# Experts ranked by count on the chip: four run in three terms on 128 slots, four in plain fp32 on 64 slots

## The reference, cut to what matters

```python
def moe_swiglu(h, w_router, b_router, w_gate, w_up, w_down):
    t = h.reshape(-1, dm)                                    # 256 x 1024
    logits = (t @ w_router).astype(jnp.float32) + b_router
    top_vals, top_idx = lax.top_k(logits, TOP_K)             # TOP_K = 2
    top_w = jax.nn.softmax(top_vals, axis=-1)
    gates = jnp.einsum('nk,nke->ne', top_w, jax.nn.one_hot(top_idx, N_EXPERTS))
    out = jnp.zeros_like(t)
    for e in range(N_EXPERTS):                               # 8
        out = out + gates[:, e:e + 1] * swiglu(t, w_gate[e], w_up[e], w_down[e])
    return out.reshape(bsz, seq, dm)
```

## Time and profile before

| | us |
|---|---|
| median of 3 runs | 1613.96 |
| lowest, highest | 1603.14, 1616.47 |
| the profiled execution, own time | 1598.46 |
| its span | 1596.6 |
| PE busy, PEld busy | 1526.7, 1222.6 |
| DVE busy, ACT busy | 1249.4, 1013.3 |

### The profile page before, as it was taken

How to read it: one execution, slowest core, us unless ns; L and a number is a source line. 1 busy time by engine, 2 the same in 40 slices (tenths; PEclk the granted TensorE clock), 3 DMA queues, 4 the chain that set the end, 5 groups by cost and what they waited for, 6 DMA issues and landing times.

```text
span 1596.6 us, 21161 instructions
## 1 busy us (share of the span) xinstructions
PE 1526.7 (96%) x7000; PEld 1222.6 (77%) x7000; DVE 1249.4 (78%) x1298; ACT 1013.3 (63%) x1181; POOL 156.2 (10%) x116
## 2 busy tenths in 40 slices
PE   7998989998999989999999999999999999999897
PEld 6866578887876657887887887887887887887685
DVE  6777564543876758888888888888888888888786
ACT  4576354343466736677777777777777777777574
POOL 0555000000154300000000000000000000000000
PEclk9999999998996999999999999999999999999899
DMA  9431254543521227999999999999999999999892
GB/s 342 171 109 34 110 211 173 190 164 117 213 106 57 89 93 271 377 370 348 395 368 365 385 368 369 377 377 364 381 370 370 379 371 366 385 370 366 346 371 88
DMA packets 68237, 442.05 MB, mean 277 GB/s; under 512 B 8416, under 2 KB 14944, under 8 KB 18528
## 3 DMA queue, kind: packets, MB, share of 16 engines
q1 hardware_dynamic: 64880, 429.60, 71.0%
q0 software_dynamic: 2304, 8.19, 1.4%
q10 hardware_dynamic: 1008, 3.67, 0.6%
HBM read 432.52 MB, written 5.77 MB: 275 GB/s over the span
## 4 chain that ended last, share of the span: by engine, by line
PE 83%; DVE 8%; DMA 4%; ACT 3%; issue 2%; SPq 0%; POOL 0%; DVEq 0%; ACTq 0%; POOLq 0%
PE ps L1660 44%; PE ps L1639 21%; DMA cw<-cmat 3%; PE ps L1437 3%; PE ps L1580 2%; PE ps L1565 2%; PE ps L1542 2%; DVE wsplit L1061 2%; PE ps L1603 2%; PE ps L1464 1%; PE ps L1494 1%; ACT wsplit L581 1%; PE ps L1475 1%; PE ps L1512 1%; PE ps L1553 1%
## 5 line engine op out<-in xcount | busy, mean ns | idle before, releaser
L1061 DVE TENSOR_TENSOR wsplit<-raw,wsplit 128x2048 fp32r<-128x2048 f32 x369 | 835.8, 2289 | 130.6 <-ACT wsplit L581 122.5
L1660 PE MATMUL ps<-wsplit,xh 128*128 128x512 f32 (+1 forms) x2144 | 707.4, 395 | 4.9 <-DVE hv L1087 3.3
L581 ACT ACTIVATE wsplit<-raw 128x2048 fp32r<-128x2048 f32 x369 | 694.2, 1914 | 2.4 <-issue 2.2
L1660 PEld LDWEIGHTS ps<-wsplit,xh 128*128 128x128 f32 x2144 | 402.7, 188 | 85.8 <-DVE wsplit L1061 3.7
L1660 PE MATMUL ps<-wsplit,xl 128*128 128x512 f32 (+1 forms) x1072 | 417.1, 389 | 0.0
L1639 PE MATMUL ps<-wsplit,hidh 128*128 128x512 f32 x1064 | 309.2, 394 | 20.2 <-DVE hidl L1068 20.2
L1639 PEld LDWEIGHTS ps<-wsplit,hidh 128*128 128x128 f32 x1064 | 200.1, 190 | 66.5 <-DVE wsplit L1061 21.0
L1660 PEld LDWEIGHTS ps<-wsplit,xl 128*128 128x128 f32 x1072 | 201.9, 188 | 38.0
L589 ACT ACTIVATE hidh<-ps 128x256 fp32r<-128x256 f32 (+1 forms) x123 | 49.7, 404 | 264.9 <-PE ps L1603 264.8
L1639 PE MATMUL ps<-wsplit,hidl 128*128 128x512 f32 x532 | 165.4, 392 | 0.0
L1639 PEld LDWEIGHTS ps<-wsplit,hidl 128*128 128x128 f32 x532 | 100.7, 189 | 21.4
(11 more groups left out here) (268 smaller groups left out, 1205.7 us busy)
## 6 DMA issues: line engine op xcount, KB each, us to landing
raw<-wffn SPq DMA_DIRECT2D x369, 1024.0 KB, 6.9
mixw<-wmix SPq DMA_DIRECT2D x12, 2048.0 KB, 8.0
cyt<-bmat SPq DMA_DIRECT2D x2, 2048.0 KB, 14.1
cw<-cmat SPq DMA_DIRECT2D x2, 2048.0 KB, 22.8
results<-ybuf ACTq DMA_DIRECT2D x7, 512.0 KB, 8.4
qk<-wglu SPq DMA_DIRECT2D x2, 1024.0 KB, 5.2
X<-x_in SPq DMA_DIRECT2D x2, 512.0 KB, 5.5
loc<-dmat SPq DMA_DIRECT2D x2, 512.0 KB, 23.3
```

The costliest lines, as they stand in the source:

```text
L581: nc.scalar.activation(wh[slot], raw[:, PLACE[slot]], ACT.Copy).then_inc(s["hi_done"], 1)
L1061: tt(wl[slot], raw[:, PLACE[slot]], wh[slot].bitcast(F32), ALU.subtract).then_inc(s["lo_done"], 1)
L1660: ins = mm(to, x2[:, fx, t * P:(t + 1) * P], of, start=(fx == 0 and i == 0), stop=(fx == KT - 1 and i == 2))
```

## The change

**Ranks.** DVE ranks the experts by count (`rank_experts`): expert 0 is put first whatever its count, the others follow by falling count. The ranks are one-hot rows (`swap`), from which DVE makes position and gate tables in rank order (`rank_tables`), and the list of expert numbers that SP reads into registers for its addresses (`order`).

**Heavy and light.** Ranks 0 to 3 are heavy: 128 slots, three terms, pieces split as before. Ranks 4 to 7 are light: 64 slots (`LCAP`), plain fp32 matmuls straight from the ring slot, with no split by ACT or DVE. A light matmul has 64 stationary columns and takes half of the piece's columns: q = 0 writes partitions 0 to 63 of a PSUM bank and q = 1 partitions 64 to 127 (`tile_position=(0, 64 * q)`). A and B are 8 such matmuls of 256 columns each, D is 4 of 512.

**In turn.** 56 rounds, one chunk of a heavy and one of a light expert in each, written out with no loop: heavy A(c), B(c), D(c-1), then light A(c-1), B(c-1), D(c-2). The split ring has five places instead of six; the ring of loads keeps six slots. A slot with a light piece is freed by the light matmuls (`light_done`), one with a heavy piece by the DVE split.

**Results.** No row goes to DRAM. After each pair of experts eight plain fp32 matmuls with the gate-weighted one-hot matrix scatter both results, one at a time through PSUM bank 7 in rounds 1 to 4 of the next pair, each followed by an add on DVE. More than 64 tokens in a light expert, or 128 in a heavy one, would give an extra pass.

The first six loads are expert 0's A0, B0, A1, B1, D0 and A2, as before. The other 330 stand behind a wait for `order_ready`, and the seventh also behind a register load of the first light expert's number.

```diff
+def load_order():
+    order = group("h", 0) + group("h", 1)
+    ahead = group("h", 2)
+    order += ahead[:1] + group("l", 0) + ahead[1:]
+    for c in range(1, CHUNKS - 2):
+        order += group("l", c) + group("h", c + 2)
+    order += group("l", CHUNKS - 2) + [("h", "D", CHUNKS - 1)] + group("l", CHUNKS - 1) + [("l", "D", CHUNKS - 1)]
+    return order
...
@@ SP
-            with sp.Fori(1, NE * 3 * NC_E // RING) as g:
-                for j in range(RING):
-                    load(j, RING * g + (base + j), RING * g + (base + j - RING + 1))
+            sp.wait_ge(s["order_ready"], 1)
+            expert = {("h", 0): 0}
+            for n, piece in enumerate(LOADS):
+                if n < RING:
+                    continue
+                kind, letter, c = piece
+                k = c // NC_E
+                if (kind, k) not in expert:
+                    e = k if kind == "h" else HEAVY + k
+                    expert[kind, k] = sp.value_load(order[0:1, e:e + 1], min_val=0, max_val=NE - 1)
+                was, its_letter, its_c = LOADS[n - RING]
+                if was == "h":
+                    sp.wait_ge(s["lo_done"], base + count(its_letter, its_c) + 1)
+                else:
+                    sp.wait_ge(s["light_done"], count(its_letter, its_c) + 1)
+                load(n % RING, expert[kind, k] * (3 * NC_E) + (base + place(letter, c)), None)
...
@@ PE
+            def light(letter, c):
...
+                if letter == "D":
+                    pe.wait_ge(s["light_hid"], c + 1)
...
+                    for n in range(2):
+                        for q in range(2):
+                            at = q * D + n * 512
+                            ins = mm(ps[LCAP * q:LCAP * q + LCAP, 4 + n], lhid[:, q], part[:, at:at + 512], start=(x == 0),
+                                     stop=(x == NC_E - 1), tile_position=(0, LCAP * q))
...
+                for f in range(4):
+                    fx = f + (4 if letter == "B" else 0)
+                    of = part[:, f * 512:(f + 1) * 512].rearrange("p (a n) -> p a n", a=2)
+                    for q in range(2):
+                        to = ps[LCAP * q:LCAP * q + LCAP, 1, 0:SEQ].rearrange("p (a n) -> p a n", a=2)
+                        ins = mm(to, xlight[:, m % 2, fx], of[:, :, q * P:(q + 1) * P], start=(fx == 0),
+                                 stop=(fx == KT - 1), tile_position=(0, LCAP * q))
+                ins.then_inc(s["light_done"], 1)
...
+            def experts():
+                for c in range(CHUNKS):
+                    m, x = divmod(c, NC_E)
+                    heavy("A", c)
+                    if c:
+                        turn_heavy(c - 1)
+                    if c > 1:
+                        turn_light(c - 2)
...
+                    if m and 1 <= x <= 4:
+                        scatter(8 * (m - 1) + 2 * (x - 1))
...
+                    heavy("B", c)
+                    if m and 1 <= x <= 4:
+                        scatter(8 * (m - 1) + 2 * (x - 1) + 1)
...
+                    if c:
+                        heavy("D", c - 1)
+                        for _, letter, at in group("l", c - 1):
+                            light(letter, at)
...
@@ ACT (DVE alike, with products, lower halves and adds in the same places)
+                    else:
+                        if c > 2:
+                            split("A", c)
+                        split("B", c)
+                        light_silu(c - 2)
+                        split("D", c - 1)
+                    if c > 1:
+                        light_hidden(c - 2)
+                    if c:
+                        hidden(c - 1)
...
+                    silu(c)
...
@@ POOL
-            for e in range(1, NE):
...
-                fetch(half[0], tokens, slot_row[:]).then_inc(s["in_rows"], 16)
...
-                    fetch(half[k], results, token_row[:, t, k:k + 1]).then_inc(s["in_results"], 16)
+            for m in range(1, HEAVY):
...
+                fetch(half[0], tokens, slot_row[:, 0:1]).then_inc(s["in_rows"], 16)
...
+                fetch(half[1][0:LCAP], tokens, slot_row[0:LCAP, 1:2]).then_inc(s["in_light_rows"], 16)
```

More of the change, by code:

```diff
@@ L128, in pieces_before, with count, place, group @@
     return 3 * NC_D + 3 * NC_E * m
-def encoder(nc, x, consts, rows, params, bmat, cmat, dmat, wmix, wglu, wrouter, wffn, tokens, results, out):
+def count(letter, c):
+    if letter == "A":
+        return 3 * c - 1 if c else 0
+    if letter == "B":
+        return 3 * c if c else 1
+    return 3 * c + 4 if c < CHUNKS - 1 else 3 * c + 2
+def place(letter, c):
+    c %= NC_E
+    if letter == "A":
+        return 3 * c - 1 if c else 0
+    if letter == "B":
+        return 3 * c if c else 1
+    return 3 * c + 4 if c < NC_E - 1 else 3 * c + 2
+def group(kind, c):
+    return [(kind, "A", c), (kind, "B", c)] + ([(kind, "D", c - 1)] if c else [])
+def load_order():
[6 more added lines that the diff above has]
+    return order
+LOADS = load_order()
+LOADED = {piece: n for n, piece in enumerate(LOADS)}
+def encoder(nc, x, consts, rows, params, bmat, cmat, dmat, wmix, wglu, wrouter, wffn, tokens, out):
     with ExitStack() as ctx:
@@ new lines, in over_expert, with middle @@
+            def over_expert(n):
+                def middle():
+                    act.wait_ge(s["o_turned"], n)
+                    nc.scalar.activation(wT[:, 0], ps[:, 7, 0:SEQ], ACT.Copy).then_inc(s["o_ready"], 1)
+                stack = Stack(n + (HEAVY - 1))
+                for j in range(AHEAD):
+                    upper(stack, j, 0)
+                act.wait_ge(s["o_gathered"], n)
+                nc.scalar.activation(xh[:, :, 0:CAP], ps[:, 4:6].rearrange("p b (a t) -> p (b a) t", a=4),
+                                     ACT.Copy).then_inc(s["o_xh"], 1)
+                stream(stack, 1, False, None, middle)
+                act.wait_ge(s["o_half"], n)
+                nc.scalar.activation(ybuf[:, 0:512], ps[:, 2], ACT.Copy).then_inc(s["o_act"], 1)
@@ L1373, in _ @@
-            expert(LAST, LAST, 0, True, False)
+            for t in range(TT):
+                ins = ts(pick[:, 0, t], cst[:, C_T:C_T + CAP], rt[:, 6, t, 0:1], None, ALU.is_equal)
+            ins.then_inc(s["picked"], 1)
+            dve.wait_ge(s["pos_done"], 2)
+            rank_experts()
+            lower(Stack(0), 2, 0)
+            nc.vector.tensor_copy(ids[:], distr.bitcast(F32).rearrange("p (a t) -> p a t", a=TT)[:, :, 0:1]
+                                  .to_broadcast([P, TT, 2]))
@@ L1808, in _ @@
+            for f in range(KT):
+                for t in range(TT):
+                    ins = mm(ps[:, 4 + f // 4, (f % 4) * P:(f % 4 + 1) * P], hn[:, t, f * P:(f + 1) * P],
+                             pick[:, 0, t], start=(t == 0), stop=(t == TT - 1))
+                if f % 4 == 3:
+                    ins.then_inc(s["gathered"], 1)
+            experts()
             pe.wait_ge(s["tables_ready"], 1)
```

721 lines of the change are left out of this document (487 added, 234 removed).

## The result

| | before | after |
|---|---|---|
| median of 4 runs each | 1614.6 us | 1503.0 us (1499.3 to 1512.5) |
| ratio, with its 95% interval | | 0.935 [0.930, 0.940] |
| profiled execution, its span | 1596.6 us | 1499.3 us, 1497.4 us |

What follows compares the result with a forecast made beforehand. The prediction took PE as the bound before and the weight stream after: first landing 607, 908 us for 329 pieces, tail 14 and coupling 9 give 1538, own time 1540, plus 5 for 1545 us; range 1465 to 1605.

Steps and rivals of the forecast that it cites:

- The price of a piece with a full queue: Weight stream behind the ranks: each 1.0486 MB piece costs 2.76 us when the queue is never empty, 329 pieces 908 us.
- two rows for 2.76: Profile readings behind the piece price: 372 GB/s over a 0.98 DMA share gave 2.76 us, four early loads' landings 2.77.
- Rival 1: Weight stream quicker when asked for more: 2.5 us a piece, PE's 821 us binds as well, total 1470 us; chance 0.13.
- the tail: After the last weight landing: light D 1.8, eviction 0.45, four scatters 3.64, then 8.3 us to the end; 14.2 in all.
- The coupling: Mutual waits between PE, the ring of loads and the stream, costed at 1% of the stage, 9 us.
- 3 us of slack a round: Ring of loads: the closest slot-release loop takes 13.7 us a round, leaving some 3 us spare against 16.6 of DMA.
- PE's round: PE's work on one heavy and one light chunk: 14.1 us, 15.9 in rounds with two scatters; light matmuls 5.24.
- What is bound: Expert stage becomes bound by the weight stream: 16.6 us of DMA a round against 14.1 of PE, which waits about 2.
- Start: Ranks to first load: ten DVE operations end at 600.2 us, register load 2 us, first load at 602.2, landing at 607.
- Rival 4: Stream can't exceed what the stage got before, 2.92 us a piece or 359 GB/s: 1598 us, no difference; chance 0.04.
- Rival 3: Ring starves, DMA idles 1 to 2 us a round or PE's clock drops: 1600 to 1655 us; chance 0.11.
- rival 2: Light matmuls' column tiles don't run side by side: 10.5 us light work, 19.3 us rounds, about 1735 us; chance 0.10.

Runs made afterwards that it cites:

- Experiment 7: Kernel before the change, with only half of each expert piece loaded from the seventh on: 1602.3 us against 1609.1 in the same series (0.996).
- experiment 3: Changed kernel with at most three weight loads in flight behind the ranks: 1520.7 us, 0.943 of before; stage 895.9 us.
- experiment 6: Changed kernel with only half of each light piece loaded: 1470.9 us, 0.912 of before; stage 850.1 us.
- Experiment 12: Changed kernel with two more loads issued ahead of the ranks and neighbouring A and B pieces asked for as one 2 MiB load: 1603.4 us, 0.995 of before.
- experiment 8: Changed kernel with half of the light experts' gate and up (A and B) matmuls left out, every piece still loaded: 1488.8 us, 0.923 of before.

## Why the prediction was right, and what was mis-sized

The profiled time is 1499.3, the forecast for it was 1540: 41 us too slow, by three terms.

- **The price of a piece with a full queue: wrong, the step that failed.** Forecast 2.76 us, 908 us for the 329, and 9 for coupling; measured 1472.8 - 609.4 = 863.4 us, coupling and all: 2.62 a piece. That is 54 us. I had two rows for 2.76, and neither holds.

The first divided 372 GB/s by the share of 0.98, as if the share measured the depth of the queue. Experiment 7 shows that this stream was paced by PE, with some 2.5 loads in flight. And 3% of its bytes were no weights: of 297 MB in the window from 700 to 1500 us, the queue of the weights moved 288.

```profile
q1 hardware_dynamic: 39582, 288.23, 94.6%
...
raw<-wffn SPq DMA_DIRECT2D x275, 1024.0 KB, 7.1
```

275 pieces in 800 us are one per 2.91. That the chain's 2.81 us, as 373 GB/s, met the window's 372 was a coincidence.

The second row took the mean of three gaps. In the trace the four loads of the earlier trace rows land at 68.8, 71.3, 74.6 and 77.0 us: gaps of 2.50, 3.31 and 2.45, so one pause and two at the full pace. The window over the larger part of their transfer:

```profile
66.00:75.00 9.00, 9.00 (x49) 7.81 (x49) 5.75 (x11) 5.74 (x16) 6.25 (x6) 1.00 1.01 425
```

1.0486 MB / 425 GB/s is 2.47 us. So the queue was full there and cheap, and the two rows agreed by chance; I took them for witnesses of each other.

The landings show the same in both kernels. In the changed one, from 660 to 1460 us, 260 of 308 gaps between landings are under 2.55 us (median 2.485, mean 2.60). Before, from 700 to 1500 us, 138 of 275 are (mean 2.91). At full pace a piece costs the same 2.49 us in both; what the change took away is pauses.
- **Rival 1** named this ("may hold waiting that is not transfer"), and its sign came: rounds under 16 us. Its price of 2.5, and that PE binds as well, are near to what was measured, so its mechanism, at a chance of 0.13, is what happened to the stream. 1503 lies below the forecast's own 1510 to 1580 and 33 us above rival 1's 1470. That the wider range held it is in part luck: it had room for the slower half of rival 1, and the tail (+10) ran against the price (-54).
- **The coupling: mis-sized the other way.** With narrow scatters a weight piece lands every 2.555 us between 660 and 1460 us. At that price the 329 pieces take 841 us, 67 less than forecast. The other 23 of the 863.4 are what I had put at 9. Of these, 13 lie in the rounds with scatters (from first to last landing the kernel with narrow scatters takes 850.5 us), and the other 10 in the start of the stage, where slots come free late (327 GB/s up to 660 us). -67 and +14 make the -54, to rounding. This rests on one profile of each. The 3 us of slack a round that I worked out for SP's loop fit experiment 3, where three loads in flight were nearly enough.
- **PE's round**: 14.1 forecast, 14.11 measured (experiment 6); 15.9 and 15.9 with scatters; light work 5.24 and 5.34; on one tile 10.5 and 10.48. But the earlier trace rows showed less than half of an overlap (0.52 us for the second eight records, 0.9 in turn), and I took the whole: that the tiles overlap fully was a guess that held, not a reading.
- **What is bound**: the stream, as forecast, in 44 of 56 rounds (rounds of 15.5 to 15.7 us instead of 16.6). In the 12 with scatters it is PE, since a stream of less than 15.7 us a round no longer covers 15.9.
- **Start**: the first load at 604.65 us instead of 602.2. `pick` ended 3.3 us later than in the trace of before, the ten operations took 2.2 us (2.1 forecast), and from the ranks to the load it was 1.0 us, not 2. +2.4 us.
- **The tail: mis-sized.** 14.2 forecast, 24.6 measured, +10.4. I had PE waiting for the last piece. It was behind: at the last landing it had 0.5 us of heavy D left, then 3.60 of light A and B and one more light D of 1.72. Also, I counted the eight records of one group of scatters (3.64) where heavy and light each have a group (3.44 + 3.65). From the first add to the end it is 9.6 us, not 8.3, and the eviction of 0.45 doesn't show. A stream cheaper than forecast leaves PE further behind, so this error and the first have one root, in part.
- **Rival 4** (the stream can't go above 2.92, and beside it the Trainium skill, DMA: Bandwidth & Descriptors, section Specifications, about 358 GB/s of HBM for each core): refuted by 408 GB/s over 800 us. Only one core ran in this case.
- **Rival 3** (the ring starves): the DMA share of 1.00 over 800 us refutes it for this kernel. Experiment 12 shows that it is real for a coarser one.

The sum: -54 for pieces with coupling, +2.4, +10.4, makes -41.

Two slips in the prediction's own text: 2.68 to 2.84 us a piece gives 1519 to 1571 by its sum, not 1510 to 1580; and its last sentence should ask for an overlap of less than a third, as rival 2 works it out.

## What to carry to other kernels

Before you take a price per transfer from a trace, ask how many were in flight: time to landing over the spacing of issues. A DMA share of 0.98 doesn't answer that. Count the transfers themselves, since GB/s holds everybody's bytes, and look at the gaps between single landings, not at their mean: in these kernels the commonest gap was the price and the rest was pauses. Two rows that agree are one witness until it is known why they agree. When a change swaps one bound for another that is within 10% of it, look for the rounds that carry extra work: they keep the old bound. And compare stages, not whole runs, when another part of the program varies by 20 us.

## What the runs showed of the hardware

- Two column tiles of 64 columns, in plain fp32, cost what one does: 32 records of 128x256 took 3.60 us on two tiles, 7.05 on one. The pair need not be adjacent in program order: with the halves one after the other, the 32 still started within 4.3 us.
- One core alone moved 1 MiB loads at 406 GB/s from three in flight on, and six were no better than three. Two gave 303 in one program and 380 in another, with a time to landing of 6.9 and 4.9 us.
- ACT's and DVE's splits and PE's matmuls beside the stream cost it at most 2.5% (2.49 to 2.52 us per MiB alone, 2.55 with all), and the common gap between landings stayed at 2.48 to 2.50 us.
- In experiment 8 PE waited 91 us of 800, and the granted clock of the window was 0.95; right after a wait of 2.83 us it was 0.50 for 5.5 us, and 12 matmuls took 5.49 us instead of 2.99. In the changed kernel PE waited 38 us of 800, and the clock was 1.00.
